# A hybrid decoder layer on one core: another rope order, a third page buffer, and prompt attention prepared in two halves

## The reference

```python
h = x @ w_in                                   # q, kc, vc, ks, vs, kw, vw, gates, ga, gb
q, ks, kw = _rope(q), _rope(ks), _rope(kw)
k_cmp = _rope(_compress(kv_all[:, :, 0], w_ck, pe_ck))   # blocks of 32 tokens, new and cached
v_cmp = _compress(kv_all[:, :, 1], w_cv, pe_cv)
o_a = _nsa_attend(q, k_cmp, v_cmp, ks, vs, kw, vw, gates)  # compressed + selected + window branch
u = ga * sigmoid(gb)
c = depthwise_conv(concat(history, u), conv_w) + conv_b    # 31 taps
c = silu(layer_norm(c))
out = concat(o_a, c) @ w_out
```

## Time and profile before

| | us |
|---|---|
| median of 3 runs | 3033.97 (3032.32 to 3037.85) |
| the profiled execution, its own time | 3037.61 |
| its span | 3035.8 |
| TensorE busy | 2748.9 |
| DVE busy | 1433.8 |
| GpSimd busy | 693.0 |
| ACT busy | 490.2 |

### The profile page before, as it was taken

How to read it: one execution, slowest core, us unless ns; L and a number is a source line. 1 busy time by engine, 2 the same in 40 slices (tenths; PEclk the granted TensorE clock), 3 DMA queues, 4 the chain that set the end, 5 groups by cost and what they waited for, 6 DMA issues and landing times. The chain is left out here.

```text
span 3035.8 us, 38687 instructions
## 1 busy us (share of the span) xinstructions
PE 2748.9 (91%) x15429; PEld 2529.0 (83%) x15429; DVE 1433.8 (47%) x2224; ACT 490.2 (16%) x710; POOL 693.0 (23%) x366
## 2 busy tenths in 40 slices
PE   8978866778889899999999999969899999999995
PEld 8978733445559799999999997969799999999983
DVE  4999036555643653333333336763643333333334
ACT  3111033223340320000000003040310000000002
POOL 3422002000002133222322221412132322233210
PEclk9987867799999999999999999979999999999998
DMA  4114560000021011111111111101011111111101
GB/s 154 57 35 135 115 194 1 0 1 1 1 87 42 22 48 42 46 44 41 41 43 47 41 41 22 49 28 49 25 46 41 41 44 46 41 41 41 48 7 59
DMA packets 82854, 145.01 MB, mean 48 GB/s; under 512 B 26382, under 2 KB 54286, under 8 KB 82446
## 3 DMA queue, kind: packets, MB, share of 16 engines
q1 hardware_dynamic: 60126, 129.68, 13.4%
q10 hardware_dynamic: 22640, 14.16, 1.6%
HBM read 134.88 MB, written 13.07 MB: 49 GB/s over the span
## 5 line engine op out<-in xcount | busy, mean ns | idle before, releaser
L581 PE MATMUL PS<-XH,WH 128*128 128x364 f32 x3048 | 682.6, 333 | 66.2 <-ACTq L1033 16.3
L581 PE MATMUL PS<-XL,WH 128*128 128x364 f32 x3048 | 678.8, 331 | 0.0
L581 PE MATMUL PS<-XH,WL 128*128 128x364 f32 x3048 | 678.5, 331 | 0.0
L536 POOL CAST WH<-RAW 128x1024 fp32r<-128x1024 f32 x177 | 206.9, 1169 | 2010.5 <-PE PS L581 1333.0
L581 PEld LDWEIGHTS PS<-XH,WH 128*128 128x128 f32 x3048 | 536.6, 190 | 68.4 <-issue 44.1
L581 PEld LDWEIGHTS PS<-XL,WH 128*128 128x128 f32 x3048 | 536.2, 190 | 0.0
L581 PEld LDWEIGHTS PS<-XH,WL 128*128 128x128 f32 x3048 | 535.5, 190 | 0.0
L538 POOL TENSOR_TENSOR WL<-RAW,WH 128x1024 fp32r<-128x1024 f32 x177 | 465.8, 2631 | 14.2
L562 PE MATMUL PS<-HH,WH 128*128 128x364 f32 x1056 | 354.0, 335 | 29.4 <-DVE Y L1800 15.1
L1800 DVE TENSOR_TENSOR Y<-Y,PS 128x364 f32<-128x364 f32 x480 | 254.1, 533 | 230.7 <-PE PS L567 225.8
L567 PE MATMUL PS<-HL,WH 128*128 128x364 f32 x1056 | 348.2, 330 | 0.0
(11 more groups left out here) (276 smaller groups left out, 2449.7 us busy)
## 6 DMA issues: line engine op xcount, KB each, us to landing
RAW<-wst SPq DMA_DIRECT2D x174, 512.0 KB, 3.3
KVP<-cache SPq DMA_DIRECT2D x64, 128.0 KB, 2.2
XRAW<-xT SPq DMA_DIRECT2D x8, 546.0 KB, 10.7
Y<-xT SPq DMA_DIRECT2D x8, 546.0 KB, 7.6
yT<-Y ACTq DMA_DIRECT2D x3, 1456.0 KB, 9.6
PG<-cache SPq DMA_DIRECT2D x64, 64.0 KB, 2.2
PG<-cache ACTq DMA_DIRECT2D x64, 64.0 KB, 2.3
win_old<-win_past SPq DMA_DIRECT2D x1, 4032.0 KB, 16.1
```

Source lines behind the costliest of these rows:

```text
L536: pool.tensor_copy(WH[:, s, :], RAW[:, s, :]).then_inc(hi_done, 1)
L581: mm = pe.matmul(PS[:, 3 * bank_set + c, 0:CH], w, x[:, k, c * CH:(c + 1) * CH], start=(q == 0 and w is hi and x is XH), stop=(q == len(ks ...
```

## The change

DVE ropes q0 after 27 taps of block 1 and the other three between taps of block 2. pe_t is loaded after tile gb2; the compression weights come in four pieces (two of 16 positions for each kind), waited for piece by piece. The four turns of vs and vw of the prompt stand between jobs 3 and 4. DVE does the key half of KR after job 2 and only the last part after job 4, and no longer waits for SMC before. A third buffer for sample pages and windows lies in the space of the weight ring; SP's third group no longer waits for the first, the fourth waits for the first; GpSimd's clearing of QLM1 waits for the third group. HIGHS, TWICE and LOWS are cut into two halves of the tokens; the second half's parts are made inside attention (ACT at `turn` 1 to 6, DVE after `cmpv` 2 to 6, GpSimd as they come), and unit `cmp` 8 waits for them. DVE makes the key rows before it centres. The diff without its unchanged lines, and without declarations of buffers and semaphores:

```diff
@@ -389,16 +393,35 @@
-        HIGHS = [(QT[HALF[g], :, 0:NP_TOK], QQ[g][HALF[g], 0:R, 0:NP_TOK]) for g in range(G)] + \
-            [(kv(name)[HALF[g], 0:NP_TOK], KE[b][g][HALF[g], :]) for b, name in enumerate(("ks", "kw")) for g in range(G)] + \
-            [(KCT[HALF[g], 0:NB], KCC[g][HALF[g], :]) for g in range(G)] + \
+        HALVES = [slice(0, NP_TOK // 2), slice(NP_TOK // 2, NP_TOK)]
+        NAMES = ("ks", "kw")
+        def highs(t):
+            return [(QT[HALF[g], :, t], QQ[g][HALF[g], 0:R, t]) for g in range(G)] + \
+                [(kv(NAMES[b])[HALF[g], t], KE[b][g][HALF[g], t]) for b in range(2) for g in range(G)]
+        SMALL = [(KCT[HALF[g], 0:NB], KCC[g][HALF[g], :]) for g in range(G)] + \
...
-        TWICE = [(QQ[g][HALF[g], 0:R, 0:NP_TOK], QQ[g][HALF[1 - g], 0:R, 0:NP_TOK], g + 1) for g in range(G)] + \
-            [(KE[b][g][HALF[g], :], KK[b][g][HALF[g], :], G + 2 * b + g + 1) for b in range(2) for g in range(G)]
-        LOWS = [(QT[HALF[g], :, 0:NP_TOK], QQ[g][HALF[g], 0:R, 0:NP_TOK], QLM[g][HALF[g], :, 0:NP_TOK], G) for g in (1, 0)] + \
-            [(kv(name)[HALF[g], 0:NP_TOK], KE[b][g][HALF[g], :], KK[b][g][HALF[1 - g], :], G + 2 * b + g + 1)
-             for b, name in enumerate(("ks", "kw")) for g in range(G)] + \
-            [(KCT[HALF[g], 0:NB], KCC[g][HALF[g], :], KCC[g][HALF[1 - g], :], 3 * G + g + 1) for g in range(G)]
+        HIGHS = highs(HALVES[0]) + SMALL + highs(HALVES[1])
+        HI_AT = [0, 3 * G + len(SMALL)]
+        TWICE = [(QQ[g][HALF[g], 0:R, t], QQ[g][HALF[1 - g], 0:R, t], at + g + 1) for t, at in zip(HALVES, HI_AT) for g in range(G)]
+        TWICE = TWICE[:G] + [(KE[b][g][HALF[g], HALVES[0]], KK[b][g][HALF[g], HALVES[0]], G + 2 * b + g + 1)
+                             for b in range(2) for g in range(G)] + \
+            TWICE[G:] + [(KE[b][g][HALF[g], HALVES[1]], KK[b][g][HALF[g], HALVES[1]], HI_AT[1] + G + 2 * b + g + 1)
+                         for b in range(2) for g in range(G)]
+        def lows(t, at):
+            return [(QT[HALF[g], :, t], QQ[g][HALF[g], 0:R, t], QLM[g][HALF[g], 0:R, t], at + G) for g in (1, 0)] + \
+                [(kv(NAMES[b])[HALF[g], t], KE[b][g][HALF[g], t], KK[b][g][HALF[1 - g], t], at + G + 2 * b + g + 1)
+                 for b in range(2) for g in range(G)]
+        LOWS = lows(HALVES[0], HI_AT[0]) + \
+            [(KCT[HALF[g], 0:NB], KCC[g][HALF[g], :], KCC[g][HALF[1 - g], :], 3 * G + g + 1) for g in range(G)] + \
+            lows(HALVES[1], HI_AT[1])
+        LO_FIRST = 3 * G + G
+        LATER_LOWS = {2: (0,), 3: (1,), 4: (2,), 5: (3, 4), 6: (5,)}
+        HI_FIRST = HI_AT[1]
+        TW_FIRST = len(TWICE) // 2
@@ -429,8 +452,9 @@
-                        eng.dma_start(CWK[:, :, :], cw_k).then_inc(cw_loaded[0], 16)
-                        eng.dma_start(CWV[:, :, :], cw_v).then_inc(cw_loaded[1], 16)
+                        for kind, (t, src) in enumerate(((CWK, cw_k), (CWV, cw_v))):
+                            for p in range(0, NB, CWP):
+                                eng.dma_start(t[:, p:p + CWP, :], src[:, p:p + CWP, :]).then_inc(cw_loaded[kind][p // CWP], 16)
@@ -510,8 +534,12 @@
-                if gi >= 2:
-                    sp.wait_ge(s_pv, 3 * (gi - 1))
+                if gi == 2:
+                    sp.wait_ge(w_split, RING + EARLY)
+                    sp.wait_ge(full["in"], N_IN)
+                    sp.wait_ge(turned, T_GATE + 1)
+                if gi == 3:
+                    sp.wait_ge(s_pv, 3)
@@ -541,12 +569,15 @@
+            pool.wait_ge(s_pv, 3 * 3)
...
-            for src, dst, ready in TWICE:
+            for n, (src, dst, ready) in enumerate(TWICE):
...
-            pool.wait_ge(q_lo, 2 * G + 1)
-            pool.memset(QLM[0][HALF[1], :, :].bitcast(F32), 0.0).then_inc(q_twice, 1)
+                if n % TW_FIRST == 1:
+                    h = n // TW_FIRST
+                    pool.wait_ge(q_lo, 2 * G + 1 + h * LO_FIRST)
+                    pool.memset(QLM[0][HALF[1], :, HALVES[h]].bitcast(F32), 0.0).then_inc(q_twice, 1)
@@ -694,30 +727,34 @@
-                pe.wait_ge(cw_loaded[kind], 16)
...
-                         lambda p: KV4[:, kind, 0:NP_TOK + NB].rearrange("q (n p) -> q n p", p=NB)[:, :, p])
-            for job in range(4):
-                kind, half = job // 2, job % 2
-                w = (CWK, CWV)[kind]
-                pe.wait_ge(cw_loaded[kind], 16)
-                pe.wait_ge(pg_loaded[half], JOB * 16 * (kind + 1))
-                mm = compress(PS[:, kind, NB + half * P:NB + (half + 1) * P], w,
-                              lambda p: PG[:, half, :, :].rearrange("q a (n p) -> q (a n) p", p=NB)[:, :, p])
-                mm.then_inc(job_done, 1)
+                         lambda p: KV4[:, kind, 0:NP_TOK + NB].rearrange("q (n p) -> q n p", p=NB)[:, :, p], cw_loaded[kind])
...
-            pe.wait_ge(kr_done, 1)
-            pe.wait_ge(roped, 6)
-            for n, (srcs, _, rows) in enumerate(TURNS):
+            def turn_in(n):
+                srcs, _, rows = TURNS[n]
...
+            for job in range(4):
+                kind, half = job // 2, job % 2
+                w = (CWK, CWV)[kind]
+                pe.wait_ge(pg_loaded[half], JOB * 16 * (kind + 1))
+                mm = compress(PS[:, kind, NB + half * P:NB + (half + 1) * P], w,
+                              lambda p: PG[:, half, :, :].rearrange("q a (n p) -> q (a n) p", p=NB)[:, :, p])
+                mm.then_inc(job_done, 1)
+                if job == 2:
+                    for n in range(4):
+                        turn_in(n)
+            pe.wait_ge(kr_done, 1)
+            pe.wait_ge(roped, 6)
+            for n in range(4, len(TURNS)):
+                turn_in(n)
@@ -825,6 +862,10 @@
+                    if m == N_PH // 2:
+                        pe.wait_ge(q_lo, len(LOWS) + 2 * G)
+                        pe.wait_ge(q_hi, len(HIGHS))
+                        pe.wait_ge(q_twice, len(TWICE) + 2)
@@ -1031,28 +1072,28 @@
+                if name == "gb2":
+                    act.wait_ge(kc_stored, 16 * 2)
+                    for kind in range(2):
+                        act.dma_start(KV4[:, kind, NP_TOK:NP_TOK + NB], pe_t[:, kind]).then_inc(pe_loaded, 16)
...
-            act.wait_ge(kc_stored, 16 * 2)
-            for kind in range(2):
-                act.dma_start(KV4[:, kind, NP_TOK:NP_TOK + NB], pe_t[:, kind]).then_inc(pe_loaded, 16)
...
-            act.wait_ge(job_done, 4)
-            act.dma_start(SMC[:, :], smp_c).then_inc(smp_c_loaded, 16)
-            sample_windows(act, 0)
...
-                if n == 0:
+                if n == 4:
...
+                if n == 3:
+                    act.wait_ge(job_done, 4)
+                    act.dma_start(SMC[:, :], smp_c).then_inc(smp_c_loaded, 16)
+                    sample_windows(act, 0)
@@ -1106,14 +1147,14 @@
-                for n in range(4 * G):
+                for n in range(3 * G):
...
-                for n in range(4 * G, len(HIGHS)):
+                for n in range(3 * G, HI_FIRST):
@@ -1205,6 +1246,8 @@
+                    if 1 <= m <= 3 * G:
+                        split_high(HI_FIRST + m - 1)
@@ -1395,41 +1438,43 @@
-            conv(1, range(CW))
+            conv(1, range(0, 27))
+            rope(QT[:, 0, :])
+            conv(1, range(27, CW))
...
-            conv(2, range(0, 12))
-            rope(QT[:, 0, :])
-            conv(2, range(12, 20))
+            conv(2, range(0, 2))
...
-            conv(2, range(20, CW))
+            conv(2, range(2, 19))
...
+            conv(2, range(19, 24))
...
-            conv(3, range(0, 8))
+            conv(2, range(24, 28))
...
-            conv(3, range(8, CW))
+            conv(2, range(28, CW))
+            conv(3, range(CW))
...
-            dve.wait_ge(job_done, 4)
...
-            dve.wait_ge(smp_c_loaded, 16)
...
-            dve.memset(VNAT[:, :, :, :, HD:HD + 1], 1.0).then_inc(v_ones, 1)
...
+            rotc = PB[:, 0, 0:nkc]
...
-                link(dve.tensor_copy(ST[:, 250 + kind:251 + kind], PS[:, kind, nkc + NB:nkc + NB + 1]))
-            for kind in range(2):
+                dve.wait_ge(job_done, 2 * kind + 2)
...
+                link(dve.tensor_copy(bias, PS[:, kind, nkc + NB:nkc + NB + 1]))
...
+                if kind == 0:
+                    for q in range(4):
+                        o = q ^ 1
+                        link(dve.tensor_copy(PB[32 * q:32 * q + 32, 0, 0:nkc], KR[32 * o:32 * o + 32, 0, :]))
...
-            rotc = PB[:, 0, 0:nkc]
-            for q in range(4):
-                o = q ^ 1
-                link(dve.tensor_copy(PB[32 * q:32 * q + 32, 0, 0:nkc], KR[32 * o:32 * o + 32, 0, :]))
+            dve.memset(VNAT[:, :, :, :, HD:HD + 1], 1.0).then_inc(v_ones, 1)
+            dve.wait_ge(smp_c_loaded, 16)
@@ -1500,10 +1545,12 @@
-            def conv_norm():
-                for c in range(NCH):
-                    centre(CA[:, :, c * CH:(c + 1) * CH], CT, 0, c)
+            def split_low(n):
+                src, hi, lo, ready = LOWS[n]
```

(46 more changed lines are left out.)

## The result

The changed kernel takes **3008.61 us** (median of 4 runs, 3005.87 to 3008.86) against 3033.14 beside it: a ratio of 0.9914, 95% interval 0.9897 to 0.9931, or 24.5 us less. The forecast was 2996 with a range up to 3006: the way was right, a good third of the gain missing. The profiled executions differ by more, 3037.61 to 3008.58, or 29.0, because the one of before lay 4.5 us above the 3033.14 (3.6 above the median shown ahead of the prediction).

The account below looks back on a forecast made before the run. Bound: weight streaming, but from about 190 to 500 us one chain of stalls, page jobs, sample groups and preparation. 27.5 + 11.7 + 2.5 - 3 = 38.7, taken as 38 off the profiled 3037.61; median 3.6 lower: 2996 us, range 2986 to 3006.

Parts of the forecast that it names:

- +3: Second half's parts made inside attention: 3 us lost, range 0 to +8, from late DVE work only partly covered by idling.
- -2.5: Start of attention: closing the idle gap lets it begin at 2.4 GHz, gaining 2.5 us, range 0 to 5.
- Rope order, pe_t, weights: Projections to compression: 16.3 us stall goes, last tile ends at 244.5, compression starts at 250.4, 26.8 us earlier.
- Jobs, turns, constants: Page jobs to first sample matmul: job 4 ends at 340.6, 26.1 us earlier; first sample matmul about 352.5, was 384.65.
- Sample pages: Four sample groups: SP stays the pace, 5 us new wait, third buffer about 1 us; stage ends 27.5 us earlier.
- Preparation in halves: Before attention: first unit at t0+23.3 against 35.0, limited by alternating squares and variances; 11.7 us gained.
- t0: The end of the last sample group, from which the forecast counted the preparation.
- if the cover were gone: Case inside attention where no idling hides DVE's late second-half parts, costing all 7.3 us.
- appeared only after idle stretches: Argument against the rival of attention at 1.2 GHz (chance 0.02): clock 0.5 was seen only after TensorE idled.
- Rival B: Attention: late halves fully on the path (7.3 us DVE, 2 ACT, some contention), clock returns nothing; 3007; chance 0.10.
- Rival A: Page jobs: SP or ACT issue pages too late, so only the tile stall's 18.6 us survives; 3004; chance 0.08.

Follow-up runs that it names:

- combined: act_pages with lows_before_ov's move, filler's extra matmuls and q2's rope moved ahead of gate 3; 2988.5 us.
- whole_prep: Changed kernel with the halves undone, all high parts, copies and low parts made before the first attention unit, key rows still first; 3008.9 us.
- two_buffers: Changed kernel with two sample page buffers and SP's old waits instead of three buffers; 3008.5 us.
- keys_after_means: Changed kernel with DVE making the key rows after the three centrings instead of before; 3010.4 us.
- filler: Changed kernel with two unneeded 512-column matmuls after each of the 11 units of attention step 0; 3003.5 us.
- old_ropes: Changed kernel with the old rope order put back; 3021.0 us.
- lows_before_ov: Changed kernel with DVE's late low parts moved from behind the value steps to before the first mix of each step; 3001.6 us.
- act_pages: Changed kernel with ACT instead of SP issuing the 16 pages of sample group 0, between the fourth turn and job 4's end; 2995.4 us.

## Why the prediction was off, step by step

The median came out 12.6 us above the forecast 2996. Between the profiled executions 38.7 was forecast and 29.0 measured. These 9.7 us are 3.8 up to the first sample matmul (steps 1 and 2), 2.1 over the sample groups (3), 0.3 in the preparation (4) and 3.5 in attention (5 and 6). To them come 3.6 from the step to the median (7), less the 0.7 by which I had rounded 38.7 down.

The step that failed most is the account of attention: "+3" for the second half and "-2.5" for the clock, a loss of 0.5 in all. Measured were 4.0 between the two profiles, and 7.7 between the kernels with and without the halves.

1. **Rope order, pe_t, weights: right, 1.7 us short.** The stall went, the last tile ended at 244.5. I had taken 1.79 us a tap from block 1; from 199.5 on they took 1.85 and then 2.0. q2's rope ended at 246.3, not 242, so the gates' copy, not the weights, set the start (252.1 for 250.4). combined, with the rope earlier, starts at 249.5.
2. **Jobs, turns, constants: right mechanism, 2 us more.** Job 3 started at 310.7 (308.2), job 4 at 328.3 (326), the first sample matmul at 356.3 (352.5). The turns hid 2.2 of the old 3.2 us of page wait; 1.0 was left.
3. **Sample pages: the waits right, the last group mis-sized, in part by chance.** 3.5 us of wait came ahead of the first group (5 forecast), and the third buffer was worth 1 us or less (none). I let the last group run in the 16.1 us that it took before, though my own range said 16.3 to 18.3, and it took 18.7. The stretch was to last 81.3 us (352.5 to 433.8) and lasted 83.4. In four other kernels with these page issues (whole_prep, two_buffers, keys_after_means, filler) the last group took 16.1 to 16.6 and the stretch 81.5 to 82.5; in two (old_ropes, lows_before_ov) it took 18.5 and 18.7 and the stretch 83.5 and 83.6. So up to 1.9 of the 2.1 us are the clock of this one profile. With the 3.8 us of late start, the means began 21.6 us earlier instead of 27.5.
4. **Preparation in halves: right.** 23.1 us from the means' start was forecast (23.3 from t0), 23.4 measured. It ends on a variance, as said. The terms of DVE were too small, the key rows with 8.12 us for 7.15 and the four KK low parts with 4.04 for 2.8, but DVE was not the limit.
5. **The second half inside attention, +3: failed in size, and in how it is paid.** In the profiles, attention takes 394.3 us in the six kernels with the halves as placed (393.8 to 394.9) and 386.6 in the four without (382.8 to 390.3): +7.7. All of it lies in the first eight steps, among which the late parts are made: 165.9 to 167.0 us with them, 155.0 to 162.3 without, and 227.8 to 229.3 for the other eight in all ten kernels. That 7.7 is near my 7.3 us "if the cover were gone" proves nothing: the cover behind the first value step held, as forecast by 2.19 us in the earlier trace rows; behind the second it did not, as 0.45 had said. What I did not price is the other half of the bill: TensorE's busy time for the same matmuls grew by 3.7 us against whole_prep, at the lower clock, and its idle time by 3.8. The better place was a pause earlier, ahead of the mixes, where DVE waits 5.7 to 6.4 us for others. lows_before_ov recovers 5.7 of the 7.7. The rest, ACT's and GpSimd's share among it, was not separated, nor why a small delay of the units costs the level.
6. **Clock, -2.5: right for 1.5 us, then wrong.** I expected attention to begin at the upper level once the idle gap was gone, and it did. But the level fell 1.5 us later, with no gap of over 1.6 us since the first variance. filler shows that the level was worth about 4 us there, near the 5 I had given as the bound. My argument that the lower level "appeared only after idle stretches" did not fit the trace I had: the third sample group of before ran at 0.59 with no gap of over 1.5 us inside it.
7. **From the profile to the median: 3.6 us.** I took the sum off the profiled execution, 3037.61, and then 3.6 more for the median. The profiled execution of after lay at its median, so nothing came off there. The attention of before, 390.3, is the longest of the four with whole preparation and 3.7 above their mean. That would account for the 3.6; it rests on one profile.

Rival B, late halves on the path and nothing back from the clock, came nearest: it gave 3007 and had a chance of 0.10. Its reason, DVE's 7.3 us counted in full, did not hold, since the first 2.29 of them were covered. Rival A, page issue swallowing the early start ahead of the jobs, did not come: the jobs waited 2.79 and 1.00 us.

The Trainium skill's rule on GpSimd and DVE (GPSIMD Engine Reference, table at the top), that they contend for SBUF when a DVE instruction has two inputs there, fits what the preparation shows: the key rows took 8.12 us for four beside two casts of 2.42 and 2.77 us. Apart, in keys_after_means, the rows took 4.97 and the casts 1.88 and 1.89.

## What to carry to other kernels

Ask of work moved into a busy stage how long the engine waits at that very place, not whether it idles somewhere near. A pause of 2.46 us hid a low part of 2.29, one of 0.45 did not hide the next, and the pauses of 5.7 to 6.4 us a little earlier hid both. Then ask what a small delay does to the clock of the matmuls behind it: here it cost as much as the waits. When a queue's issuing is the pace, buffers behind it gain nothing until another queue takes part of it; the third buffer was worth 0 and then 9 us. Take from a profile of before only durations of work whose clock will be the same. And where the same group takes 16.1 us in one profile and 18.7 in the next, a step of 2 us read from a single profile is no finding.

## What the runs showed of the hardware that was not expected

- The granted clock of TensorE fell to its lower level (1.2 GHz) without a long idle gap: 1.00 through the variances and the first 1.5 us of attention, then 0.50. TensorE had been idle 1.01 us ahead of attention and 1.57 us at most since the first variance, and was busy 10.59 of the first 14.81 us. With fillers the clock was 1.00 there and TensorE busy 13.26 of 14.62. The Trainium skill (TensorE: Matmul & The Clock Gate, section on why this matters) advises against idle gaps between bursts; here closing the gap was not enough.
- The same 186 or so matmuls of a sample group took 15.7 to 18.8 us, going with a mean clock of 0.84 down to 0.59, both with and without a wait ahead of them.
- Four 64x1024 tensor_tensor of DVE took 8.12 us beside two casts of GpSimd and 4.97 with GpSimd idle.
- Sixteen DMAs whose addresses come from registers kept their queue busy for 12.7 to 14.2 us from first to last issue, with 4.6 to 5.0 us of reading ahead: on ACT as on SP. That, and not what the DMAs moved, set the pace of four groups: act_pages moves the same bytes and waits for none.
